# 384 instead of 416 tokens dense in the experts, 160 by gathered rows; coefficients in PSUM; ScalarE rounding the down weights

## What is computed

```
s_top, i_top = lax.top_k(sc, PEER_TOPK)          # two lists per head, from q normalised
f_s, f_pos = lax.top_k(cand, PEER_TOPK)          # of the 16 x 16 sums
gate = softmax(f_s)                              # 8 x 16 = 128 slots per token
a = einsum('td,tkd->tk', x, u_tab[eidx])
y = einsum('tk,tkd->td', gate * gelu(a), v_tab[eidx])
```

## Time and profile before

| | us |
|---|---|
| median of 3 runs | 4913.03 (4910.26 to 4913.61) |
| profiled execution: its span | 4916.6 |
| up to select | 2432 |
| select | 491 |
| gates | 798 |
| experts | 1172 |
| tail | 24 |

### The profile page before, as it was taken

One profiled execution on the slowest core, in us unless ns is written; L12 is line 12 of the kernel. 1 busy time (PEld: TensorE's weight loads), 2 busy tenths in 40 slices (PEclk: granted clock), 3 DMA queues, 4 the chain that ended last, 5 costly groups with the idle time before them and its releaser, 6 DMA issues.

```text
span 4916.6 us, 78844 instructions
## 1 busy us (share of the span) xinstructions
PE 4838.2 (98%) x32224; PEld 4723.2 (96%) x32224; DVE 3264.3 (66%) x4242; ACT 1497.5 (30%) x2899; POOL 2844.3 (58%) x1650
## 2 busy tenths in 40 slices
PE   8999999999999999999999999999999999999998
PEld 8999999999998879998999999999999999999998
DVE  5877777774423534217577777666666899999855
ACT  5333333332423432102312126666662000000001
POOL 7200000003333435555277879998997999999976
PEclk9999999999999999999999999999999999999999
DMA  7334334335343536523444449999998888888852
GB/s 275 116 126 131 126 127 128 124 127 149 107 155 127 205 131 229 186 91 128 131 141 141 141 157 333 337 335 336 335 333 295 302 315 305 305 313 302 314 181 104
DMA packets 343207, 1013.06 MB, mean 206 GB/s; under 512 B 39728, under 2 KB 132112, under 8 KB 307232
## 3 DMA queue, kind: packets, MB, share of 16 engines
q1 hardware_dynamic: 165776, 526.23, 32.0%
q0 software_dynamic: 36864, 268.45, 14.5%
q10 hardware_dynamic: 140208, 213.34, 12.1%
HBM read 882.26 MB, written 126.76 MB: 205 GB/s over the span
## 4 chain that ended last, share of the span: by engine, by line
PE 91%; DVE 4%; DMA 2%; ACT 1%; POOL 1%; issue 1%; ACTq 0%; POOLq 0%; DVEq 0%; SPq 0%
PE ps L248 21%; PE ps L252 21%; PE ps L250 21%; PE ps L761 7%; PE ps L762 7%; PE ps L760 7%; PE ps L2821 1%; PE ps L1153 1%; PE ps L1593 1%; PE ps L1170 1%; DMA ex_gate<-gate 0%; DVE in_sums L681 0%; PE ps L1559 0%; PE ps L2516 0%; PE ps L1856 0%
## 5 line engine op out<-in xcount | busy, mean ns | idle before, releaser
L218 POOL TENSOR_SCALAR w_hi<-w_raw 128x1024 fp32r<-128x1024 f32 x678 | 788.7, 1163 | 1908.5 <-PE ps L762 1079.7
L221 POOL TENSOR_TENSOR w_lo<-w_raw,w_hi 128x1024 fp32r<-128x1024 f32 x678 | 1695.8, 2501 | 56.5
L248 PE MATMUL ps<-h_hi,w_hi 128*128 128x416 f32 (+1 forms) x3552 | 1051.1, 330 | 1.0 <-ACT later_beside L410 1.0
L252 PE MATMUL ps<-h_hi,w_lo 128*128 128x416 f32 (+1 forms) x3552 | 1034.3, 326 | 0.0
L250 PE MATMUL ps<-h_lo,w_hi 128*128 128x416 f32 (+1 forms) x3552 | 1026.4, 323 | 0.0
L248 PE MATMUL ps<-ex_c_hi,w_hi 128*128 128x416 f32 x2048 | 719.4, 351 | 4.5 <-DVE ex_y L3121 2.5
L252 PE MATMUL ps<-ex_c_hi,w_lo 128*128 128x416 f32 x2048 | 723.8, 353 | 0.0
L250 PE MATMUL ps<-ex_c_lo,w_hi 128*128 128x416 f32 x2048 | 716.2, 350 | 0.0
L248 PEld LDWEIGHTS ps<-h_hi,w_hi 128*128 128x128 f32 x3552 | 622.8, 188 | 8.9 <-issue 4.8
L250 PEld LDWEIGHTS ps<-h_lo,w_hi 128*128 128x128 f32 x3552 | 622.2, 188 | 6.2
L252 PEld LDWEIGHTS ps<-h_hi,w_lo 128*128 128x128 f32 x3552 | 619.9, 188 | 2.4
(11 more groups left out here) (373 smaller groups left out, 9258.2 us busy)
## 6 DMA issues: line engine op xcount, KB each, us to landing
w_raw<-weights SPq DMA_DIRECT2D x906, 512.0 KB, 4.0
up<-up_out ACTq DMA_DIRECT2D x128, 208.0 KB, 6.6
gate<-g_sb_g ACTq DMA_DIRECT2D x13, 2048.0 KB, 13.4
proj<-rows_out ACTq DMA_DIRECT2D x97, 272.0 KB, 2.9
ex_up<-up ACTq DMA_DIRECT2D x16, 832.0 KB, 6.9
ex_gate<-gate ACTq DMA_DIRECT2D x16, 832.0 KB, 16.9
sp_first<-proj ACTq DMA_DIRECT2D x48, 272.0 KB, 3.6
sp_first<-up ACTq DMA_DIRECT2D x15, 832.0 KB, 7.2
```

Source lines behind the costliest of these rows:

```text
L218: pool.tensor_scalar(self.whi[:, to, :], self.raw[:, slot, :], 1.0, 1.0, ALU.mult, ALU.mult).then_inc(self.hi_done, 1)
L221: pool.tensor_tensor(self.wlo[:, to, :], self.raw[:, slot, :], self.whi[:, to, :].bitcast(F32), ALU.subtract).then_inc(self.split_done, 1)
L248: pe.matmul(acc, hi, x, start=first, stop=False)
L252: mm = pe.matmul(acc, lo, x, start=False, stop=last)
```

## The change

- **Split of tokens.** 384 tokens go dense (12 tiles, 384 columns in every up and down matmul). 128 go by rows as before. The other 32 are *folded*: laid out four times over the 128 partitions (`COPIES`), each copy with 4 of every 16 slots, so that 32 gathers (`FOLD_SLOTS`) serve them, 160 in all for each table. Their 32 dots run at the start of the experts, their 32 down rows go last, into a sum in SBUF (`folded`), which PE adds up over the four copies before the last set.
- **Order.** Up blocks: 4 before the heads, 5 per head, 7 per tile. Gathers are counted in one series (`place`), with 3 row buffers in gates and 5 in experts; the experts have 6 or 7 row steps a set, 13 in two.
- **Select** scores the raw queries with keys scaled by the gain, and applies the inverse root to the 16 best sums alone; POOL adds the squares and PE sums them with one column per tile.
- **Coefficients** are formed in PSUM: ACT copies up into bank 4 (`take`), DVE multiplies by the gate in place, ACT rounds, DVE subtracts. Three banks are left for the result.
- **Rounding** of the down weights (`ACT_ROUNDS`, from the fifth on) moves from POOL to ACT; POOL rounds all others and subtracts all.
- The up scratch is laid out by set, so that a partition's terms are one run.

```
-TD = 416
+TD, AT_FOLD, AT_ROWS = 384, 384, 416
+FOLD_SLOTS = SLOTS // COPIES
-UP_HEAD = 6
-UP_FIRST = 2
+UP_HEAD = 5
+UP_FIRST = 4
-GATHERS = 3
-DOWN_SLOTS = 5
+GATES_ROWS, GATES_RING = 203904, 3
+UNITS_GATES, UNITS = SLOTS + GATES_RING, 2 * (SLOTS + FOLD_SLOTS)
+ACT_ROUNDS = frozenset(i for i in range(AT_UP_GATES + RING, N_PIECES)
+                       if i >= AT_DOWN + RING)
...
+    def round_by_act(self, act, i):
+        act.wait_ge(self.raw_loaded[i % RING], 16 * (i // RING + 1))
+        act.wait_ge(self.piece_used, i - RING + 1)
+        act.activation(self.whi[:, self.halves_at(i % RING), :], self.raw[:, i % RING, :], ACT.Copy).then_inc(self.act_hi_done, 1)
     def split_piece(self, pool, slot, i, turn):
...
+        if i in ACT_ROUNDS:
+            pool.wait_ge(self.act_hi_done, act_rounds_to(i + 1))
+        else:
+            pool.tensor_scalar(self.whi[:, to, :], self.raw[:, slot, :], 1.0, 1.0, ALU.mult,
+                               ALU.mult).then_inc(self.hi_done, 1)
...
     def add_down(self, dve, u, folded):
+        coefs, total = (self.fold_coef, folded) if "fold" in name else (self.coef, self.token_rows)
...
+        dve.scalar_tensor_tensor(total, rows, c, total, ALU.mult, ALU.add).then_inc(self.rows_used, 1)
...  stage_select
-                dve.reciprocal(rstd[:, :], std[:, :]).then_inc(*dve_s.did("rstd"))
-                for c in range(KC):
-                    dve.scalar_tensor_tensor(qn[:, c, :], q[:, c, :], core.gain[:, G_PEER + c:G_PEER + c + 1],
-                                             rstd[:, :], ALU.mult, ALU.mult).then_inc(*dve_s.did(f"qn{c}"))
+                dve.reciprocal(rstd[:, :], std[:, :]).then_inc(*dve_s.did("rstd"))
+                dve.tensor_tensor(over[:, :, :], over[:, :, :], rstd[:, :].unsqueeze(2).to_broadcast(spread),
+                                  ALU.mult).then_inc(*dve_s.did("over"))
...  Coefs
+    def bank(self, G, c):
+        return self.core.ps[:, 5 if G == 0 and c % 2 else 4, 0:TD]
+    def take(self, act, G, c, up):
+        act.activation(self.bank(G, c), up[:, c, :], ACT.Copy).then_inc(self.taken, 1)
+    def weigh(self, dve, G, c, gate):
+        dve.tensor_tensor(by_tile(self.bank(G, c)), by_tile(self.bank(G, c)), gate[:, :, c * G_TILE:(c + 1) * G_TILE],
+                          ALU.mult).then_inc(self.weighed, 1)
...  stage_gates
-                while s < SLOTS and 6 * (s - GATHERS) <= 5 * n:
+                while u < UNITS_GATES and 5 * (u - GATES_RING) <= 4 * n:
...
+            token_rows(hi_fold, lo_fold)
...  stage_experts
+WEIGH_AT, REST_AT = {0: 0, 3: 1, 6: 2, 9: 3}, {2: 0, 5: 1, 8: 2, 11: 3}
+UNITS_BEFORE_FIRST = 3
+        places += [(G, j) for j in ((1, 4, 7, 10, 12, 13, 15) if G % 2 else (1, 4, 7, 10, 12, 14))]
+        bank = lambda G, j: ps[:, 7 - (KD * G + j) % 3, 0:TD]
-                        free = (added, KD * G + j - 3)
+                        free = ended["scalar"] if G == 0 and j == 1 else (added, KD * G + j - 2)
...
+            def round_weights(G, k):
+                i = down_at(G) + k + RING
+                if i < N_PIECES:
+                    core.round_by_act(act, i)
...
-        "up": [N_KEYS, P, TD]}
+        "up": [N_SETS, P, VSET, TD]}
```

More of the change, by code:

```diff
@@ L91, with act_rounds_to @@
 OQ_SCRATCH_AT, OQ_X_AT = 71808, 154752
+ACT_ROUNDS = frozenset(i for i in range(AT_UP_GATES + RING, N_PIECES)
+                       if i >= AT_DOWN + RING)
+def act_rounds_to(i):
+    return sum(1 for k in range(AT_UP_GATES, i) if k in ACT_ROUNDS)
 LOWEST = -3.0e38
@@ new lines, in __init__, with place @@
+        self.rows = [rows[:, s, :] for s in range(GATES_RING)]
+    def place(self, u):
+        if u < UNITS_GATES:
+            return u % GATES_RING, u // GATES_RING + 1, u - GATES_RING + 1
+        order = [(SLOTS + n) % GATES_RING for n in range(GATES_RING)] + [GATES_RING, GATES_RING + 1]
+        at, turn = (u - SLOTS) % len(order), (u - SLOTS) // len(order)
+        before = sum(1 for k in range(UNITS_GATES) if k % GATES_RING == order[at])
+        return order[at], turn + (before if at < GATES_RING else 1), u - len(order) + 1 if turn else 0
@@ new lines, in slot_of, with gather @@
+    def slot_of(self, u):
+        for first, count, name in ((0, SLOTS, "u"), (SLOTS, FOLD_SLOTS, "fold u"), (SLOTS + FOLD_SLOTS, SLOTS, "v"),
+                                   (2 * SLOTS + FOLD_SLOTS, FOLD_SLOTS, "fold v")):
+            if first <= u < first + count:
+                return name, u - first
+    def gather(self, pool, u):
+        at, _, used = self.place(u)
+        name, s = self.slot_of(u)
+        expert = self.fold_expert if "fold" in name else self.expert
+        if needed(used):
+            pool.wait_ge(self.rows_used, used)
+        pool.indirect_dma_start(
+            self.rows[at], None, self.core.io[f"peer_{name[-1]}"],
+            bass.IndirectOffsetOnAxis(ap=expert[:, s:s + 1], axis=0),
+        ).then_inc(self.gathered[at], 16)
@@ new lines, in wait_rows, with dot_up @@
+    def wait_rows(self, dve, u):
+        at, turn, _ = self.place(u)
+        dve.wait_ge(self.gathered[at], 16 * turn)
+        return self.rows[at]
+    def dot_up(self, dve, u):
+        rows = self.wait_rows(dve, u)
+        name, s = self.slot_of(u)
+        dots = self.fold_coef if "fold" in name else self.coef
+        if s == 0:
+            dve.wait_ge(self.x_ready, 2 if "fold" in name else 1)
+        dve.scalar_tensor_tensor(rows, rows, 1.0, self.token_rows, ALU.mult, ALU.mult,
+                                 accum_out=dots[:, s:s + 1]).then_inc(self.rows_used, 1)
@@ L2734, in round_first @@
[L2734 to L2742 removed]
+        both = core.nc.alloc_sbuf_tensor_at("ex_c", [P, 2, 2, VSET, TD], F32R, offset=self.AT)
@@ L3059, in _ @@
+            load_terms(1)
+            act.wait_ge(sparse.rows_used, SLOTS)
+            act.activation(sparse.coef[:, :], sparse.coef[:, :], ACT.Gelu).then_inc(sparse.gelu_done, 1)
+            for k in range(4):
+                round_weights(0, k)
+            load_terms(2)
+            for c in range(VSET):
+                take(1, c)
+                round_coef(1, c)
+                round_weights(0, 4 + c)
+            take(2, 0)
+            for G in range(1, LAST):
                 if G + 2 < N_SETS:
```

737 lines of the change are left out of this document (415 added, 322 removed).

## The result

The changed kernel takes **4794.31 us** (median of four runs, 4791.27 to 4800.04) against 4911.65 for the kernel before (four runs): ratio **0.9761**, 95% interval 0.9747 to 0.9775. The forecast was 4775, in a range of 4728 to 4845: the sign and the range held, and 20 of the 138 us forecast did not come.

What follows compares the result with a forecast made beforehand. PE, busy 98% of the span, bounds the kernel. Columns -173.3, other PE work -5.4, gates +6, entering experts +5, folded rows +10, DMA +20 sum to -138 us: 4775 us, range 4728 to 4845.

Steps and rivals of the forecast that it cites:

- Columns: Up and down matmuls: 32 fewer columns make each 14.1 ns shorter, -173.3 us over 12,288 matmuls.
- the forecast's other end: Up and down matmuls: time falls in proportion to the columns, 14.5 ns each, -178.6 us.
- Select: Select stage: a head takes PE 45.5 us, from 59; DVE, POOL and ScalarE stay under that, nothing lost.
- Not all of that shows: Gates: POOL exceeds PE by 2.4 us a tile, 28 in all, but only +6 us (0 to 28) is lost.
- Entering the experts: Start of experts: ScalarE's copy, folded dots on DVE and POOL's wait for stores cost +5 us (0 to 15).
- Coefficients in PSUM: Experts: products and remainders cost DVE 0.58 us like adds, nothing lost; rival of no speedup, 4906 us, chance 0.03.
- a wait of 0.7 is the mean: Folded down rows, experts: SBUF updates wait 0.7 us each for POOL's subtractions, 22 us in all, mostly slack; +10 us.
- The bound of 55: Folded down rows, experts: upper end of the loss, 0 to 55 us after DVE's spare time in five sets.
- DMA: Experts' transfers: 12.6 MB in 33.6 us needs 375 GB/s over 29 sets; +20 us taken.
- at a full share that is 378, enough: Experts' transfers: the gates' 367 GB/s at share 0.97 scales to 378 at full share, so +0 us.
- The rivals at 335 and 307 GB/s: Experts' DMA: held at the gates' rate, 4871 us, chance 0.10; or at the experts' old rate, about 4970, chance 0.05.
- POOL and ScalarE in the experts: Experts: POOL needs 28.4 and ScalarE 13.5 of 33.6 us a set, so neither delays PE; no loss.

Runs made afterwards that it cites:

- e4: Changed kernel with coefficients formed in SBUF again, in one buffer, from the second set on: 4837.01 us, ratio 0.9841.
- e1: Changed kernel with the folded tokens' down rows added first, in PSUM, and copied once to SBUF: 4762.62 us, ratio 0.9688.
- e9: Changed kernel with SyncE loading 1.05 MB more a set in the experts, into two unread buffers in turn: 4844.20 us, ratio 0.9861.
- e3: Changed kernel with GpSimd rounding all weights again and ScalarE none: 4889.99 us, ratio 0.9949.

## Why the prediction was right, and where it was off

**Columns: right, a little small.** The forecast spacing was 174.8 ns, measured 173.2 in the experts: 0.451 ns per column, against 0.454 at 416 columns. The time went in proportion (the forecast's other end), not along the flatter slope from 272 to 416. Over 6144 matmuls that is 10 us more. The Trainium skill's formula of six cycles and one per column ("VectorE: DVE Perf Modes", section on the TRN2 errata), which the prediction weighed, would give 162.5 ns at 384, an estimate from that page at 2.4 GHz. The row shows 173.2 at a granted clock of 1.00, so the formula is too low here, as it was at 416.

**Select: right.** Four blocks and eight heads at 45.5 us are 398; measured 398.7, PE busy all of it.

**Gates: the step that failed is "Not all of that shows", +6.** Its own numbers were right: POOL's tile was forecast at 66.4 us and took 66.7; PE needs 64.0. That is 32 us over twelve tiles. The prediction let most of it vanish in the 18 us that PE had lost before and in POOL's three pieces of lead. But the losses at the start stayed (8.8 us in the first twelfth of the stage), and a lead is spent once. By the prediction's own count (4032 x 0.1748, 96 x 0.66 and 7 for the token rows, 775) PE lost 42 us in place of 24: **18 short**.

**Entering the experts: +5, should have been 13.** The prediction saw 5 us of old loss and added 5; PE lost 17.6 us before 3720, against the 10 allowed, 2.4 of them to the lower clock after its gap. It looked at DVE's dots and POOL's waits for the stores; what counted was the DMA, at a share of 1.04 with gathers for five row buffers, and ScalarE's new roundings, waiting for late weights, ahead of the coefficients.

**Coefficients in PSUM: right.** 0.56 and 0.55 us against 0.58 forecast; e4 gives the price of the other way, 43 us of the whole time.

**Folded rows: +10, measured 30, of which e1 took off 26.** The step that failed is "a wait of 0.7 is the mean". It let an update wait for one subtraction's rest, by chance. In fact it waited 1.65 us in the mean and up to 5.0, since gathers hold it up as well and POOL's next instructions can go first; and the in-order adds behind it are what PE waits for. Some 6 of the 30 are the lower clock that follows PE's longer gaps, which no term of the prediction had. The bound of 55 held.

**DMA: +20, measured nothing.** The end that came true is "at a full share that is 378, enough"; the DMA gave 379 over 605 us, and 398 outside the stops. The rivals at 335 and 307 GB/s fall. The Trainium skill's figure of about 358 GB/s ("DMA: Bandwidth & Descriptors", section Specifications), one core's half of a bandwidth that two share, by which the term was 45, doesn't bind here. The Trainium skill ("HBM Reference", section Specifications) gives a core that streams alone about 425. The 398 lies between. But e9 shows that there was luck in it: 8% more bytes cost some 50 us.

**POOL and ScalarE in the experts: nothing, right**, and only because ScalarE rounds: e3 prices that at 96 us.

Together: from -138, 18 (gates), 8 (entry) and 20 (folded rows) to be added, 20 (DMA) and 10 (columns) to be taken off: -122, where the spans differ by 122.7 with 3.2 lost ahead of select. The forecast was saved by losses that stood in for each other: 30 us for DMA and folded rows in sum were right, in their shares not.

## What to carry to other kernels

When the bottleneck engine gets faster, recompute each neighbour's time per tile against the new pace, and where one is over, charge the whole difference times the tiles: a lead of a few pieces does not hide a rate. A sum that DVE updates from SBUF beside a busy GpSimd belongs in PSUM, if need be early and then copied once. And of two late inputs to one in-order queue, mending one shows little until both are mended.

## What was not expected of the hardware

A DVE update with two operands in SBUF was, by its times, passed by two further POOL instructions while it waited, and a gather's issue behind it took 2.82 us for 0.95. A gap of PE's cost more than its length: after that of 13.2 us the granted clock was 0.5 for another 5.7 us of matmuls, 0.32 us apart for 0.173. In the sets the DMA gave 398 to 400 GB/s at a share of 1.02, and every second set it ran nearly dry for some 4 us, because one engine's queue stood before the last terms to land. And stages that no edit touched ran 4 to 12 us longer in both profiles of one program than in those of others made from it, with 41 us at the lower clock for 24 to 31.
